# Second recurrent mixer of a two-block model: products of the rate phase moved from VectorE to GpSimd, on one core

## The chip, the cores and the metric

One core of a Trainium2 chip runs the whole program. The metric is the device time of one launch in microseconds, the median over repeated runs.

## The reference, cut to what matters

The program computes two blocks in float32. The second block has three mixers side by side; the second of them is a recurrent one ("rwkv7"), run forwards and backwards over 256 context and 512 latent tokens (768 columns in all). Before its scan it computes, for each direction d, a decay, a sigmoid `a`, a key `k_d` and a removal key `hd(a) * kk`; the readout at the end uses the sum of both directions' keys for a bonus term:

```
for d, (wd, ad) in enumerate(((wdf, adf), (wdb, adb))):
    w = -softplus(-(w0[d] + tanh(wd) @ w_up[d])) - 0.5
    decay = exp(-exp(w))
    a = sigmoid(a0[d] + ad @ a_up[d])
    k_d = k * (1.0 + (a - 1.0) * k_a)
    dirs.append((hd(decay), hd(k_d), hd(a) * kk))
...
bonus = (sum(r * (k_f + k_b) * r_k, axis=-1, keepdims=True) * v)
```

What follows (a chunked form of the scan, the output projection, then a mixture of 32 experts) is untouched.

## The kernel before

All tiles have 128 partitions. A feature tile of this mixer holds two halves m = 0, 1 (two heads each) of 768 columns: `kk` (normalised key), `k_` (key), `ak` (first the sigmoid `a`, then the removal key), `kd` (the key of the direction), `lw` (the sigmoid of the decay), `ci` and `ce` (running sums of `lw` within chunks of 128, with and without the own column), `e_tot` (the chunks' totals), `bias` (columns of the sums that centre later exponentials). `bonus` holds the latent part (512 columns) of the keys, summed over directions.

`rwkv_direction` (L3230) handles one direction. Its first stage is a weave of two programs: the chain of `rwkv_rates` (L3264) and `rwkv_decays` (L3324, with `rwkv_scores` L3591 woven into it), and as filler `early_project` (L1586), a part of the output projection (multiplications L1608, additions to x by VectorE L1615, weights loaded by the SP queue). `weave` (L395) opens a stage with barriers at both ends and writes each engine's instructions in the order of the fractions that the programs yield. The chain is put together by `in_turn` (L106): at the end of a part each of its computing engines drains and adds to the semaphore "ended", and every engine that has work in the next part waits until all have:

```
if i:
    eng.wait_ge(sem["ended"], sum(len(c) for c in computing[:i]))
...
    eng.drain().then_inc(sem["ended"], 1)
```

The engines of one stage share an order of work only by semaphores. `Chain` (L52), called `link`, makes an engine wait for the instruction that it has just issued, so that the next one may read its result.

In `rwkv_rates` TensorE multiplies four times (L3276), ScalarE takes sigmoids (L3287) into `lw` and `ak`, and VectorE makes the running sums (L2449), then per half the key of the direction in two steps (L3300 tensor_scalar, L3301 scalar_tensor_tensor), one product of both halves of `ak` with `kk` (L3302), the bonus (L3304 a copy in direction 0, L3306 an addition in direction 1), and per half the totals (L3309, a copy of 6 columns) and differences or sums of 768 columns (L3311 in direction 0; L3313 and L3314 in direction 1), last four small biases (L3318, L3319). GpSimd has nothing in it. In `rwkv_decays` ScalarE starts with L3350 and VectorE with L3332; L3338 reads `ak`, the transposes of TensorE (L3374) wait for it, and GpSimd's first work is L3718 of `rwkv_scores`, beside VectorE's L3673 and L3674.

Lines of other stages that are named below: L771 and L775 (VectorE, rotary products of the first block) and L253 (GpSimd, sums of weights there), L225 and L2239 (GpSimd products), L1797 and L2131 (GpSimd copies), L2611 (VectorE, tensor_scalar of 768 columns) and L2631 (VectorE, the copy of totals) in the first mixer.

Of the kernel before, what the change touches and what calls it, by code (L numbers as in the profile page):

```python
# [16 lines left out]
ALU = mybir.AluOpType  # L17
# [5 lines left out]
CTX = 256  # L23
# [1706 lines left out]
def over_heads(ap, n=HD):  # L1730

    shape = list(ap.shape) + [n]
    return ap.unsqueeze(len(ap.shape)).broadcast_to(shape)
# [712 lines left out]
def running_sums(nc, K, dve, link, lw, cum, tiles):  # L2446

    for t in tiles:
        link(nc.vector.tensor_tensor_scan(cum[:, t], K.reset[:], lw[:, t], 0.0, ALU.mult, ALU.add))  # L2449


def chunks(ap):

    return ap.rearrange("p (c n) -> p c n", n=P)
# [775 lines left out]
def rwkv_direction(nc, K, d, up_w, r_, k_, p_mix, kk, v_T, bonus, y, filler, rep, end):  # L3230
# [10 lines left out]
    with ExitStack() as p2:  # L3241
        kd, ak, lw = sb("kd", [P, 2, T2], p2), sb("ak", [P, 2, T2], p2), sb("lw", [P, 2, T2], p2)
        both = sb("c", [P, 2, 2, T2], p2)
        ce, ci = both[:, 0], both[:, 1]
        bias = sb("bias", [P, 2, 2, 3 * NCH], p2)
        chain = in_turn(
            (15, rwkv_rates(nc, K, d, up_w, p_mix, kk, k_, kd, ak, lw, ci, ce, e_tot, bias, bonus, range(4))),
            (54, rwkv_decays(nc, K, kk, r_, kd, ak, lw, ci, ce, at, kke, koT, re, e_tot, range(6),
                             rwkv_scores(nc, K, d, r_, kk, kd, ak, both, bias, at, bt, cd, (lw[:], p_mix[:, 4:6]), p_mix[:, 8], range(6)))))
        weave(nc, f"ru{d}", chain, filler)  # L3250
# [13 lines left out]
def rwkv_rates(nc, K, d, up_w, p_mix, kk, k_, kd, ak, lw, ci, ce, e_tot, bias, bonus, banks):  # L3264

    rows = slice(d * HD, (d + 1) * HD)
    border = HD - 1 if d == 0 else HD
    pieces = ((0, S), (S, CTX))

    def tensor(eng, sem):  # L3270
        for j in range(4):
            yield j / 8
            if j >= 2:
                eng.wait_ge(sem["sig"], j - 1)
            for x, (at_, n) in enumerate(pieces):
                ins = nc.tensor.matmul(K.psum[:, banks[2 * (j % 2) + x], :n], up_w[rows, j // 2, (j % 2) * P:(j % 2 + 1) * P],  # L3276
                                       p_mix[rows, 6 + j // 2, at_:at_ + n], start=True, stop=True)
            ins.then_inc(sem["up"], 1)

    def scalar(eng, sem):  # L3280
        eng.preload_act_table_set(SIGMOID)
        for j in range(4):
            yield (j + 0.5) / 8
            eng.wait_ge(sem["up"], j + 1)
            first = 10 + 4 * (j // 2) + 2 * d + j % 2
            for x, (at_, n) in enumerate(pieces):
                ins = nc.scalar.activation((lw, ak)[j // 2][:, j % 2, at_:at_ + n], K.psum[:, banks[2 * (j % 2) + x], :n], ACT.Sigmoid, bias=K.rw[:, first:first + 1])  # L3287
            ins.then_inc(sem["sig"], 1)
        eng.preload_act_table_set(LOG_EXP)

    def vector(eng, sem):
        link = Chain(eng, sem["v"])
        for m in range(2):
            yield 0.2 + 0.1 * m
            eng.wait_ge(sem["sig"], m + 1)
            running_sums(nc, K, eng, link, lw, ci, [m])
        yield 0.5
        for m in range(2):
            eng.wait_ge(sem["sig"], 3 + m)
            link(nc.vector.tensor_scalar(kd[:, m], ak[:, m], -1.0, K.rw[:, 6 + m:7 + m], ALU.add, ALU.mult))  # L3300
            link(nc.vector.scalar_tensor_tensor(kd[:, m], kd[:, m], 1.0, k_[:, m], ALU.add, ALU.mult))  # L3301
        link(nc.vector.tensor_tensor(ak[:], ak[:], kk[:], ALU.mult))  # L3302
        if d == 0:
            nc.vector.tensor_copy(bonus[:], kd[:, :, CTX:])  # L3304
        else:
            nc.vector.tensor_tensor(bonus[:], bonus[:], kd[:, :, CTX:], ALU.add)  # L3306
        yield 0.8
        for m in range(2):
            link(nc.vector.tensor_copy(e_tot[:, m], chunks(ci[:, m])[:, :, P - 1]))  # L3309
            if d == 0:  # L3310
                link(nc.vector.tensor_tensor(ce[:, m], ci[:, m], lw[:, m], ALU.subtract))  # L3311
            else:
                link(nc.vector.tensor_tensor(chunks(ce[:, m]), over_heads(e_tot[:, m], P), chunks(ci[:, m]), ALU.subtract))  # L3313
                link(nc.vector.tensor_tensor(ci[:, m], ce[:, m], lw[:, m], ALU.add))  # L3314
        middle = ci.rearrange("p m (c n) -> p m c n", n=HD)[:, :, :, 31]
        edge = ci.rearrange("p m (c n) -> p m c n", n=P)[:, :, :, border]
        for x, rate in enumerate((-RATE, RATE)):
            nc.vector.tensor_scalar(bias[:, x, :, 0:2 * NCH], middle, rate, None, ALU.mult)  # L3318
            nc.vector.tensor_scalar(bias[:, x, :, 2 * NCH:3 * NCH], edge, rate, None, ALU.mult)  # L3319

    return Program(["up", "sig", "v"], tensor=tensor, scalar=scalar, vector=vector)


def rwkv_decays(nc, K, kk, r_, kd, ak, lw, ci, ce, at, kke, koT, re, e_tot, banks, scores):  # L3324
# [1208 lines left out]
```

## Time and profile before

| | us |
|---|---|
| median of 3 runs (lowest, highest) | 2134.77 (2133.16, 2139.09) |
| the profiled execution | 2135.21 |
| its span in the trace | 2133.0 |
| busy: TensorE, VectorE, ScalarE, GpSimd | 1978.6 (93%), 987.5 (46%), 619.2 (29%), 354.7 (17%) |
| mean granted TensorE clock, share of full | 0.966 |

The profiled execution's time is 2.2 us more than its span, for what lies around the first and the last instruction. Busy shares are averages over stages. The timeline lists instructions by their start in us from the beginning of the span, with the idle time of the engine before them and what ended it; PE is TensorE, PEld its weight loads, DVE VectorE, ACT ScalarE, POOL GpSimd, and a q behind a name means the engine's sequencer (waits, drains, branches).

### The profile page before, as it was taken

The numbers are of one execution on the slowest core, as the hardware profiler recorded it, in microseconds if no ns is written. First come the engines' busy times: TensorE is split into PE (matmuls) and PEld (weight loads), VectorE is DVE, ScalarE is ACT, GpSimd is POOL, SyncE is SP. The second block draws the span as 40 slices with busy tenths as digits, with TensorE's granted clock in tenths as the row PEclk, the third lists the DMA queues.
The fourth block names the chain that finished last, engine by engine and source line by source line (L and its number), as shares of the span: only waits on it lengthen the run. The fifth ranks groups of instructions, "written<-read, shape, count | busy, mean of one in ns | idle before, by whom it ended". The sixth has DMA issues, their size and how long they took to land. (4 is left out here: it accounts for less than half of the span.)

```text
span 2133.0 us, 32611 instructions
## 1 busy us (share of the span) xinstructions
PE 1978.6 (93%) x13378; PEld 1387.4 (65%) x13378; DVE 987.5 (46%) x1954; ACT 619.2 (29%) x1311; POOL 354.7 (17%) x301
## 2 busy tenths in 40 slices
PE   7999999988999999998998898897899999999996
PEld 5885768856566576686996654684795555445542
DVE  5772075724452425478635777748743222111013
ACT  4551162131122212443123165326213111111111
POOL 5442103202220233341003100201300000000001
PEclk9999999979899999999999999899899999999999
DMA  4222201200001873121113110000018999999997
GB/s 168 89 83 79 79 18 51 71 25 30 30 27 40 330 290 135 40 79 31 41 46 118 32 37 30 2 2 31 3 30 349 396 426 427 426 425 426 428 427 314
DMA packets 51795, 325.84 MB, mean 153 GB/s; under 512 B 6464, under 2 KB 9152, under 8 KB 33344
## 3 DMA queue, kind: packets, MB, share of 16 engines
q1 hardware_dynamic: 50352, 319.03, 38.1%
q0 software_dynamic: 1152, 4.19, 0.5%
q8 instruction: 108, 1.77, 0.3%
q10 hardware_dynamic: 144, 0.52, 0.1%
q14 instruction: 39, 0.32, 0.0%
HBM read 311.67 MB, written 9.96 MB: 151 GB/s over the span
## 5 line engine op out<-in xcount | busy, mean ns | idle before, releaser
L3992 PE MATMUL psum<-m_ring,m_xg 128*64 128x512 f32 x944 | 207.1, 593 | 8.9 <-DMA m_ring<-in_w_in 8.9
L3992 PEld LDWEIGHTS psum<-m_ring,m_xg 128*64 128x64 f32 x944 | 68.4, 137 | 143.7 <-issue 143.6
L3974 PEld LDWEIGHTS psum<-m_sel,m_htok 128*128 128x128 f32 x1024 | 118.3, 194 | 13.7 <-issue 12.2
L3974 PE MATMUL psum<-m_sel,m_htok 128*128 128x128 f32 x1024 | 122.7, 279 | 1.4 <-DVE m_sel L3965 1.4
L3998 ACT ACTIVATE rstd<-psum 64x512 f32<-64x512 f32 x32 | 18.8, 588 | 302.8 <-PE psum L3992 288.3
L4002 DVE TENSOR_TENSOR m_hid<-rstd,psum 64x512 f32<-64x512 f32 x32 | 22.1, 691 | 171.6 <-ACT rstd L3998 171.5
L4017 PE MATMUL psum<-m_ring,m_hid_t 128*64 128x512 f32 x432 | 96.4, 596 | 2.3 <-DMA m_ring<-in_w_down 1.6
L4089 POOL DMA_INDIRECT m_ring<-expert_rows,m_pos x8 | 8.7, 1088 | 478.1 <-DMA expert_rows<-tmp 476.0
L289 PE MATMUL psum<-h,wring 128*128 128x256 f32 x336 | 82.9, 391 | 3.8 <-POOL n_v L262 1.9
L444 PE MATMUL psum<-wring,h 128*128 128x128 f32 x704 | 83.5, 277 | 0.7 <-ACT n_k L350 0.5
L829 PE MATMUL psum<-wring,h 128*128 128x512 f32 x192 | 82.6, 592 | 0.0
L444 PEld LDWEIGHTS psum<-wring,h 128*128 128x128 f32 x704 | 80.2, 192 | 2.6 <-ACT n_k L350 0.9
L746 ACT ACTIVATE tmp<-gatedB 32x512 f32<-32x512 f32 x96 | 60.3, 628 | 62.6 <-DVE gatedB L357 61.4
L289 PEld LDWEIGHTS psum<-h,wring 128*128 128x128 f32 x336 | 65.2, 196 | 19.2 <-issue 8.1
L829 PEld LDWEIGHTS psum<-wring,h 128*128 128x128 f32 x192 | 51.6, 269 | 30.5 <-issue 15.1
L1331 PE MATMUL psum<-h,wring 128*128 128x512 f32 x128 | 66.4, 650 | 0.8 <-ACT rstd L1341 0.8
L4017 PEld LDWEIGHTS psum<-m_ring,m_hid_t 128*64 128x64 f32 x432 | 29.5, 137 | 57.1 <-issue 51.9
L289 PE MATMUL psum<-v,folds 128*128 128x256 f32 x264 | 60.6, 379 | 0.1
L4023 DVE TENSOR_TENSOR tmp<-psum,rows 128x512 f32<-128x512 f32 x16 | 11.1, 691 | 106.2 <-DMA expert_rows<-tmp 102.6
L289 PE MATMUL psum<-x,wring 128*128 128x256 f32 x240 | 57.0, 380 | 2.0 <-DVE g_xc L357 2.0
L3965 DVE TENSOR_TENSOR m_sel<-m_rank,m_count 128x256 f32<-128x256 f32 x32 | 12.2, 421 | 99.9 <-PE psum L3974 99.6
L3983 ACT ACTIVATE m_xg<-psum,mod,gains 128x128 f32<-128x128 f32 x128 | 48.0, 459 | 30.9 <-PE psum L3974 30.9
(761 smaller groups left out, 4212.0 us busy)
## 6 DMA issues: line engine op xcount, KB each, us to landing
m_ring<-in_w_in SPq DMA_DIRECT2D x59, 2048.0 KB, 27.4
m_ring<-in_w_down SPq DMA_DIRECT2D x54, 1024.0 KB, 27.5
wring<-in_w1f SPq DMA_DIRECT2D x60, 512.0 KB, 3.5
ada_ring<-in_w_ada SPq DMA_DIRECT2D x12, 2048.0 KB, 12.2
wring<-in_w2f SPq DMA_DIRECT2D x31, 512.0 KB, 3.4
x<-in_w_in SPq DMA_DIRECT2D x5, 2048.0 KB, 24.7
x<-in_w_down SPq DMA_DIRECT2D x10, 1024.0 KB, 30.0
expert_rows<-tmp SPq DMA_DIRECT2D x14, 512.0 KB, 28.3
```

The source lines that it names most:

```text
L289: m = nc.tensor.matmul(self.bank(q, name)[:, :CTX], lhs(k), rhs(k), start=(fresh and k == 0), stop=(k == half - 1), skip_group_check=True)
L444: return nc.tensor.matmul(place(t, out), lhs, rhs, start=(k == 0), stop=(k == KD - 1))
L746: m = nc.scalar.activation(K.tmp[to:to + quarter, t % 2], of[p0:p0 + quarter], ACT.Copy)
L829: m = nc.tensor.matmul(K.psum[:, banks[u]], tokens, weights[:, kk], start=(k == 0), stop=(k == KD - 1))
L1331: m = nc.tensor.matmul(K.psum[:, banks[i % 2]], ws.weights(first + i, k), (h, gated)[i % 2][:, k], start=(k == 0), stop=(k == nk - 1))
L3965: return nc.vector.tensor_tensor(W.sel[:, :, s], over_heads(rank_e, SLOTS), over_rows(slots, TT), ALU.is_equal)
L3974: m = nc.tensor.matmul(K.psum[:, GATHER + k // 4, at:at + n], h_tok[:, t, k * P:(k + 1) * P], W.sel[:, t].rearrange("p s n -> p (s n)")[:, ...
L3983: m = nc.scalar.activation(W.xg[:, k].rearrange("p s n -> p (s n)")[:, :n], K.psum[:, GATHER + k // 4, at:at + n], ACT.Identity, scale=pre ...
L3992: m = nc.tensor.matmul(K.psum[i * SLOTS:(i + 1) * SLOTS, UP + s], W.xg[:, k, s], w[i], start=(k == 0), stop=(k == KD - 1))
L3998: return nc.scalar.activation(W.sg[s][SLOTS:], K.psum[0:SLOTS, UP + s], ACT.Silu)
L4002: return nc.vector.tensor_tensor(W.hid[s * SLOTS:(s + 1) * SLOTS], W.sg[s][SLOTS:], K.psum[SLOTS:, UP + s], ALU.mult)
L4017: m = nc.tensor.matmul(K.psum[at, DOWN + dh], W.hid_t[:, f, at], w[:, f], start=(f == 0), stop=(f == FT - 1))
```

## The change

Per half, the product of `ak` and `kk` goes to GpSimd as soon as VectorE's tensor_scalar has read `ak` (semaphore "less"), and the bonus as soon as `kd` is ready (semaphore "keys"), copied or added per half. VectorE's two links in the key's steps become a wait on "less" and a signal "keys", and it goes on to the totals. The phase now has four computing engines for "ended".

```diff
         for m in range(2):
             eng.wait_ge(sem["sig"], 3 + m)
-            link(nc.vector.tensor_scalar(kd[:, m], ak[:, m], -1.0, K.rw[:, 6 + m:7 + m], ALU.add, ALU.mult))
-            link(nc.vector.scalar_tensor_tensor(kd[:, m], kd[:, m], 1.0, k_[:, m], ALU.add, ALU.mult))
-        link(nc.vector.tensor_tensor(ak[:], ak[:], kk[:], ALU.mult))
-        if d == 0:
-            nc.vector.tensor_copy(bonus[:], kd[:, :, CTX:])
-        else:
-            nc.vector.tensor_tensor(bonus[:], bonus[:], kd[:, :, CTX:], ALU.add)
+            nc.vector.tensor_scalar(kd[:, m], ak[:, m], -1.0, K.rw[:, 6 + m:7 + m], ALU.add, ALU.mult).then_inc(sem["less"], 1)
+            eng.wait_ge(sem["less"], m + 1)
+            nc.vector.scalar_tensor_tensor(kd[:, m], kd[:, m], 1.0, k_[:, m], ALU.add, ALU.mult).then_inc(sem["keys"], 1)
         yield 0.8
...
-    return Program(["up", "sig", "v"], tensor=tensor, scalar=scalar, vector=vector)
+    def gpsimd(eng, sem):
+        yield 0.5
+        for m in range(2):
+            eng.wait_ge(sem["less"], m + 1)
+            nc.gpsimd.tensor_tensor(ak[:, m], ak[:, m], kk[:, m], ALU.mult)
+        yield 0.8
+        for m in range(2):
+            eng.wait_ge(sem["keys"], m + 1)
+            of = kd[:, m, CTX:]
+            if d == 0:
+                nc.gpsimd.tensor_copy(bonus[:, m], of)
+            else:
+                nc.gpsimd.tensor_tensor(bonus[:, m], bonus[:, m], of, ALU.add)
+
+    return Program(["up", "sig", "less", "keys", "v"], tensor=tensor, scalar=scalar, vector=vector, gpsimd=gpsimd)
```

## Rows read from the trace of the kernel before

**Rows 1.** Timeline, direction 0: start us, us, engine, line, operation, tiles, count [idle <-releaser].

```profile
1306.22 0.62 DVE L3300 TENSOR_SCALAR r_kd<-r_ak,vecs 128x768 f32<-128x768 f32 x1
...
1306.88 0.96 DVE L3301 SCALAR_TENSOR_TENSOR r_kd<-r_kd,p_mix 128x768 f32<-128x768 f32 x1
...
1309.52 1.76 DVE L3302 TENSOR_TENSOR r_ak<-r_ak,late 128x1536 f32<-128x1536 f32 x1
1311.31 0.69 DVE L3304 COPY r_bonus<-r_kd 128x1024 f32<-128x1024 f32 x1
1311.92 0.16 DVE L3309 COPY r_etot<-r_c 128x6 f32<-128x6 f32 x1
...
1313.32 0.96 DVE L3311 TENSOR_TENSOR r_c<-r_c,r_lw 128x768 f32<-128x768 f32 x1
...
1314.81 1.48 ACT L3350 ACTIVATE r_kke<-r_c 128x1536 f32<-128x1536 f32 x1 [6.92 <-DVEq L128]
```

**Rows 2.** Timeline, direction 1.

```profile
1450.89 1.76 DVE L3302 TENSOR_TENSOR r_ak<-r_ak,late 128x1536 f32<-128x1536 f32 x1
1452.68 1.22 DVE L3306 TENSOR_TENSOR r_bonus<-r_bonus,r_kd 128x1024 f32<-128x1024 f32 x1
1453.83 0.16 DVE L3309 COPY r_etot<-r_c 128x6 f32<-128x6 f32 x1
...
1458.70 1.48 ACT L3350 ACTIVATE r_kke<-r_c 128x1536 f32<-128x1536 f32 x1 [9.43 <-DVEq L128]
```

**Rows 3.** Single lines of GpSimd: duration in ns (min/median/max), first and last start, shape.

```profile
L2239 POOL TENSOR_TENSOR g_pool<-g_pool,const x8: 1260/1268/1272, 503.8 to 551.9; 128x512 f32<-128x512 f32 x8
...
L225 POOL TENSOR_TENSOR x<-h x1: 2353/2353/2353, 163.4 to 163.4; 128x1024 f32<-128x1024 f32 x1
...
L1797 POOL COPY g_pool<-level x1: 397/397/397, 559.0 to 559.0; 128x256 f32<-128x256 f32 x1
...
L2131 POOL COPY x<-g_g x1: 1887/1887/1887, 469.8 to 469.8; 128x2048 f32<-128x2048 f32 x1
```

**Rows 4.** Timeline, the first block at 31 to 35 us.

```profile
31.22 1.64 DVE L775 TENSOR_TENSOR qk<-qk,tmp 128x512 f32<-128x512 f32 x1
...
32.39 1.60 POOL L253 TENSOR_TENSOR folds<-folds,wring 128x512 f32<-128x512 f32 x1
...
32.79 1.75 DVE L771 TENSOR_TENSOR qk<-gatedB,rstd 128x512 f32<-128x512 f32 x1
```

**Rows 5.** Timeline, the phase behind the rates, direction 0.

```profile
1321.77 1.59 POOL L3718 TENSOR_TENSOR r_lw<-r_kd,p_mix 128x256 f32<-128x256 f32 x1 [124.91 <-DVE r_at L3338]
...
1326.23 1.02 POOL L3718 TENSOR_TENSOR r_lw<-r_kd,p_mix 128x256 f32<-128x256 f32 x1 [2.46 <-ACT p_mix L3636]
1326.24 0.42 DVE L3673 TENSOR_TENSOR r_lw<-r_ak,p_mix 128x256 f32<-128x256 f32 x1
...
1326.58 0.82 DVE L3674 TENSOR_TENSOR r_lw<-r_ak,p_mix 128x128 f32<-128x128 f32 x1
```

**Rows 6.** Single lines of VectorE, columns as in rows 3.

```profile
L775 DVE TENSOR_TENSOR qk<-qk,tmp x24: 691/1368/3110, 31.2 to 175.4; 128x512 f32<-128x512 f32 x24
...
L2611 DVE TENSOR_SCALAR h_k<-h_k,vecs x4: 619/1082/1510, 907.8 to 936.5; 128x768 f32<-128x768 f32 x4
...
L2631 DVE COPY h_etot<-h_c x2: 171/614/1056, 952.8 to 955.9; 128x6 f32<-128x6 f32 x2
```

**Rows 7.** Stretches: length, then busy us per engine (x instructions), PEclk, DMA share, GB/s.

```profile
1309.50:1314.80 5.30, 0.00 (x0) 0.00 (x0) 5.06 (x10) 0.00 (x0) 0.00 (x0) 0.75 0.00 0
1314.80:1318.40 3.60, 3.56 (x4) 1.52 (x5) 3.53 (x3) 3.22 (x4) 0.00 (x0) 0.50 0.03 7
1321.70:1325.00 3.30, 3.05 (x25) 2.81 (x26) 3.30 (x5) 2.43 (x7) 2.00 (x2) 1.00 0.00 0
1451.00:1458.70 7.70, 0.00 (x0) 0.00 (x0) 7.40 (x12) 0.00 (x1) 0.00 (x0) 0.79 0.00 0
1458.70:1462.30 3.60, 3.58 (x5) 1.51 (x6) 3.54 (x3) 3.23 (x4) 0.00 (x0) 0.50 0.00 0
```

## The prediction

> **What bounds the kernel now.** Over the whole span TensorE is the busy engine, 93% against 46% for VectorE and 17% for GpSimd (the table above), but that is an average over stages, and the change touches two short phases: the rates of direction 0, at about 1300 to 1315 us, and those of direction 1, at about 1441 to 1459 us. I therefore read the timeline of these two phases first, then looked for places where GpSimd and VectorE already work at once, and last at TensorE's clock around the phases.
>
> In the timeline the reader is to see who is late. After the projections and sigmoids only VectorE works: from 1306.22 one instruction follows the other, the second difference (L3311) ends at 1314.28, four small biases follow, and ScalarE's first instruction of the next phase (L3350) starts at 1314.81, 0.53 after that difference, having had 6.92 us of idle time that VectorE ended [rows 1]. In direction 1 the same ScalarE line starts at 1458.70 after 9.43 us of idleness that VectorE ended [rows 2]. TensorE does nothing from 1309.5 to 1314.8 and from 1451 to 1458.7 [rows 7]. So each microsecond of VectorE in this phase is a microsecond of the kernel, and the phase boundary (every computing engine adds to "ended", everyone waits) hands it on whole. GpSimd is free: its first work in the next phase (L3718) is where VectorE's L3338 is what it waits for, 124.91 us of idle time before it [rows 5]. That is the case for the move. The case against it is that the moved instructions read SBUF, as does nearly all that stays on VectorE.
>
> **What goes away on VectorE.** In direction 0 the product of ak and kk (L3302) starts at 1309.52 and the first copy of totals (L3309) at 1311.92: 2.40 us start to start, for L3302 (1.76) and L3304 (0.69) [rows 1]. In direction 1 it is 1450.89 to 1453.83: 2.94 us for L3302 (1.76) and L3306 (1.22) [rows 2]. Together 5.34. Two waits of VectorE on itself also fall away per direction. A linked instruction starts 0.03 to 0.04 us after its predecessor ends (L3301 at 1306.88 after 1306.84), an unlinked one 0.08 before it (L3309 at 1311.92, the copy before it ends at 1312.00) [rows 1]: 0.1 us each, 0.2 per direction, 0.4 in all.
>
> **What comes to GpSimd.** Per direction two products over 128x768 and two bonus operations over 128x512. A GpSimd product of 512 columns takes 1.27 us and one of 1024 takes 2.35 [rows 3], so 2.11 ns per column and 1.27 + 256 x 2.11 ns = 1.81 for 768. Its copy takes 0.397 for 256 columns and 1.887 for 2048 [rows 3], so 0.83 ns per column and 0.61 for 512. Direction 0: 2 x 1.81 + 2 x 0.61 = 4.84. Direction 1, where the bonus is a sum, 2 x 1.81 + 2 x 1.27 = 6.16. The Trainium skill (GPSIMD Engine Reference, Performance versus the Vector engine) gives some 2.6 cycles per column for two inputs at 1.2 GHz, an estimate of 1.66 us for 768 columns; by it each of the four would be 0.15 shorter, 0.6 in all, and the sum below +2.6. The rows' durations are the ones used.
>
> **Do they run side by side?** The trace answers this. VectorE's L775, a product of two 512-column SBUF operands, takes 0.691 at its shortest [rows 6]. With GpSimd at work L775 takes 1.64 and L771 1.75, and GpSimd's L253 takes 1.60 in place of 1.27 [rows 4]. The ends tell how: L775 ends at 32.86, L253 at 33.99, 1.13 later; L771 then ends at 34.54, 0.55 later. Each ends its own duration less 0.14 after the other's end. That is turn by turn, with 0.14 of start-up hidden, and not a common slowing. The stage right behind the rates shows it too: GpSimd's L3718, the same product each time, takes 1.59 at 1321.77 and 1.02 at 1326.23, by what VectorE has under way; L3674, that comes while it lasts, takes 0.82, although L3673 with twice its columns takes 0.42 [rows 5]. So VectorE's next instruction doesn't pass a GpSimd one that already waits. The one-input forms are no exception: the tensor_scalar of 128x768 takes 0.62 free and up to 1.51 beside GpSimd, and the tiny copy of totals, 128x6, took 1.06 instead of 0.17 [rows 6]. So totals, differences, sums and both steps of kd all meet GpSimd in turns.
>
> The Trainium skill (SBUF — State Buffer, Who interferes with whom) states that VectorE and GpSimd share a port pair, that whoever starts first holds it for the whole instruction and the other fully blocks. That rule speaks against this change. The trace agrees on the turns, but it hides 0.14 us at each hand-over; blocking with nothing hidden would give +5.7 us in place of the sum below. The measurement decides.
>
> **Schedule of direction 0** (end times; "held" ends at the end before it plus its duration less 0.14). Tensor_scalar m0 1306.84. L3301 m0 starts at 1306.88, before GpSimd has reacted, and ends 1307.84. GpSimd product m0, held, 1309.51. Tensor_scalar m1, held, 1309.99. L3301 m1 1310.99. GpSimd product m1 1312.66. Totals m0 1312.69. GpSimd bonus copy m0 1313.16. Difference m0 1313.98. GpSimd copy m1 1314.45. Totals m1 1314.48, difference m1 1315.48, and 0.53 from there to the next phase as now: 1316.0 in place of 1314.81. **+1.2 us.**
>
> **Direction 1.** Tensor_scalar m0 1448.22 (as long before L3302's old start as in direction 0), L3301 m0 1449.21, GpSimd product m0 1450.88, tensor_scalar m1 1451.36, L3301 m1 1452.36, GpSimd product m1 1454.03, totals m0 1454.06, GpSimd sum m0 1455.19, L3313 m0 1456.01, GpSimd sum m1 1457.14, L3314 m0 1457.96, totals m1 1458.16, L3313 m1 1459.16, L3314 m1 1460.16, next phase at 1460.7 in place of 1458.70. **+2.0 us.**
>
> As a check: 4.84 + 6.16 of GpSimd time, less 5.34, less some 17 hand-overs at 0.14 (2.4), is +3.2. The dropped waits give nothing here, since VectorE stands behind GpSimd at that moment. The ends of this term, by rows: nothing contended, -5.34 - 0.4 = -5.7 (GpSimd would finish at about 1311.7 and 1454.4, ahead of VectorE at 1312.1 and 1455.5, so it is covered); nothing hidden, 11.00 - 5.34 = +5.7. I take +3.2, since the rows with the same forms show turns with 0.14 hidden.
>
> **The small edits.** GpSimd now drains and adds to "ended", and the count waited for rises by one. In the schedule it ends 1 us and 3 us before VectorE, which hides it; with that cover gone it costs a hand-over of about 0.1. The new wait of VectorE on "less" has the place of the old link. Behind GpSimd's waits nothing else is queued in these phases, and no DMA moves: SP's weight loads and the output projection's multiplications keep their place. I take 0, between -0.1 and +0.3 for both directions.
>
> **TensorE's clock.** During the idle time it falls; from the restart it is granted 0.50 (1.2 GHz) for 3.6 us in both directions, after 5.3 us of idleness and after 7.7 [rows 7]. A longer pause before it changes nothing in that, and at 1321.7, where the transposes on the path begin, it is at 1.00 again (2.4 GHz). The matmuls in the slow stretch are the output projection's and are not waited for. I take 0.
>
> **Sum.** 2135.21 (profiled execution, span 2133.0) + 3.2 = 2138.4. The median of the runs shown, 2134.77, is 0.4 lower, so I expect a median of **2138.0**, +0.15%. About 0.3% (6.4 us) is what a measurement of this kernel can tell from no change; the three runs of before span 5.9 us alone.
>
> **Rivals.**
> (a) Turns as forecast, between nothing hidden and some extra hiding, +1 to +5.7: 2136 to 2140.5. Chance 0.81.
> (b) The instructions fit beside each other: -5.7, 2129.1. For it: the engines have no data in common but two handed-over tiles, and L3718 beside one-input work isn't slowed everywhere. Against it are the turns, for each of the forms that stay on VectorE [rows 4 to 6]. It decides if L3301 and L3311 keep 0.96 us beside a GpSimd product. Chance 0.08; it would be a gain of 0.27%, so about half of it would be read as faster.
> (c) Half of it: contention for the products only, while the totals and differences run beside the bonus work; GpSimd 2 x 3.62 = 7.24 less 5.34 less 8 hand-overs (1.1) = +0.8: 2135.6. Against it is the 1.06 us copy [rows 6]. Chance 0.07.
> (d) Slower past the bound: TensorE's pause, lengthened by 1.2 and 2.0, keeps the low clock until the transposes at 1321.7 and 1465.6. PE is busy 3.05 us in that stretch at full clock [rows 7]; at half it would be about twice that, +3 per direction, 2138.0 + 6 = 2144. It decides if the granted clock is still 0.50 more than 6.9 us after the restart. Against it: 3.6 us after either pause. Chance 0.04.
>
> **How the numbers follow.** (a) is the likeliest and sets 2138.0. The range takes in (a), (c) and the spread of runs on either side of their median (-1.6, +4.3), and leaves out (b) and (d): 2131.5 to 2142.0. Faster by over 0.3%: half of (b), 0.04. Slower by over 0.3%: (d) and the top of (a) with a high run, 0.05. Within: 0.91.
>
> **What would show it.** Right: GpSimd's products last 2.3 to 2.7 us where they arrive behind L3301 (1.81 alone); tensor_scalar of m1 lasts over 2 us instead of 0.62; the copy of totals of m0 about 1.7 instead of 0.16; L3350 starts about 1.2 and 2.0 us later after the phase's first sigmoid. Wrong: L3301, L3311, L3313 and L3314 at 0.96 throughout and L3350 2.6 to 3.1 earlier; or GpSimd as the engine that L3350 waits for; or any change of length in a stage outside the two phases.

## The result, and the profile after

The changed kernel takes 2136.74 us in the median of 20 runs (2133.05 to 2142.28) and the kernel before 2131.14 in 20 runs (2125.29 to 2139.09); the ratio is 1.0019 with a 95% interval of 1.0010 to 1.0028. That is slower by 2 to 6 us, and within the 0.3% that the prediction called no change. The median of before is now 3.6 us under that of the first three runs, so the ratio (+0.15% forecast, +0.19% measured) says more than a comparison of 2136.74 with the forecast 2138.0.

The profiled execution took 2135.00 us (span 2132.8; before 2133.0). Two single executions can't be set against each other by their spans: in this one the first running sum of the phase came almost 5 us earlier than in the profile of before, with nothing changed ahead of it. The phases themselves can. The busy shares first, from section 1 of the page after: GpSimd has eight instructions more and 15.5 us more busy time, VectorE four fewer and yet 2.8 us more, because an instruction that waits for its turn is recorded as running, as the rows below show.

```profile
PE 1979.3 (93%) x13378; PEld 1388.3 (65%) x13378; DVE 990.3 (46%) x1950; ACT 619.5 (29%) x1311; POOL 370.2 (17%) x309
```

The timeline of direction 0 of the changed kernel, columns as in rows 1 (L3302 is now the second key step, L3305 the totals, L3307 the difference, L3321 GpSimd's product, L3327 its bonus copy, L3360 ScalarE's first instruction of the next phase):

```profile
1301.30 0.62 DVE L3300 TENSOR_SCALAR r_kd<-r_ak,vecs 128x768 f32<-128x768 f32 x1
...
1301.95 0.96 DVE L3302 SCALAR_TENSOR_TENSOR r_kd<-r_kd,p_mix 128x768 f32<-128x768 f32 x1
1302.00 2.58 POOL L3321 TENSOR_TENSOR r_ak<-r_ak,late 128x768 f32<-128x768 f32 x1 [107.73 <-DVE r_kd L3300]
...
1302.83 2.16 DVE L3300 TENSOR_SCALAR r_kd<-r_ak,vecs 128x768 f32<-128x768 f32 x1
...
1305.03 0.96 DVE L3302 SCALAR_TENSOR_TENSOR r_kd<-r_kd,p_mix 128x768 f32<-128x768 f32 x1
1305.07 2.57 POOL L3321 TENSOR_TENSOR r_ak<-r_ak,late 128x768 f32<-128x768 f32 x1 [0.50 <-DVE r_kd L3300]
1305.90 1.77 DVE L3305 COPY r_etot<-r_c 128x6 f32<-128x6 f32 x1
1307.59 1.89 POOL L3327 COPY r_bonus<-r_kd 128x512 f32<-128x512 f32 x2
1307.70 1.30 DVE L3307 TENSOR_TENSOR r_c<-r_c,r_lw 128x768 f32<-128x768 f32 x1
1309.04 0.46 DVE L3305 COPY r_etot<-r_c 128x6 f32<-128x6 f32 x1
1309.54 0.96 DVE L3307 TENSOR_TENSOR r_c<-r_c,r_lw 128x768 f32<-128x768 f32 x1
...
1311.03 1.48 ACT L3360 ACTIVATE r_kke<-r_c 128x1536 f32<-128x1536 f32 x1 [8.07 <-DVEq L128]
```

The reader is to see the turns. GpSimd's first product comes 0.05 us behind L3302, lasts 2.58 instead of 1.81, and ends 1.66 after L3302 does. The tensor_scalar of m1, 0.62 in [rows 1], lasts 2.16; the copy of six columns of totals 1.77 instead of 0.16. From the first tensor_scalar to ScalarE's L3360 it is 9.74 us, where rows 1 have 8.59. The same in direction 1 (L3309, L3310 differences and sums, L3329 the bonus sum):

```profile
1447.84 2.16 DVE L3300 TENSOR_SCALAR r_kd<-r_ak,vecs 128x768 f32<-128x768 f32 x1
...
1450.91 1.77 DVE L3305 COPY r_etot<-r_c 128x6 f32<-128x6 f32 x1
1452.61 3.19 POOL L3329 TENSOR_TENSOR r_bonus<-r_bonus,r_kd 128x512 f32<-128x512 f32 x2
1452.71 1.97 DVE L3309 TENSOR_TENSOR r_c<-r_etot,r_c 128x768 f32<-128x768 f32 x1
1454.72 1.90 DVE L3310 TENSOR_TENSOR r_c<-r_c,r_lw 128x768 f32<-128x768 f32 x1
...
1459.35 1.48 ACT L3360 ACTIVATE r_kke<-r_c 128x1536 f32<-128x1536 f32 x1 [11.37 <-DVEq L128]
```

Here the phase takes 13.04 us in place of 11.10. The difference and the sum of m0 last 1.97 and 1.90 instead of 0.96, each behind one of GpSimd's bonus sums (two merged in the row, 3.19 together). The two phases give **+1.15 and +1.94, 3.1 us in all**.

Last TensorE's clock in the changed kernel, columns as in rows 7:

```profile
1311.05:1316.60 5.55, 5.54 (x7) 2.42 (x8) 5.51 (x4) 5.18 (x10) 0.00 (x0) 0.50 0.12 36
...
1317.80:1321.00 3.20, 2.84 (x24) 2.60 (x25) 3.20 (x6) 2.33 (x7) 2.01 (x2) 1.00 0.00 0
1400.00:1406.00 6.00, 6.00 (x32) 6.00 (x32) 0.00 (x0) 1.92 (x4) 0.00 (x0) 0.55 0.00 0
...
1459.36:1463.40 4.04, 4.04 (x5) 1.85 (x6) 4.00 (x3) 3.67 (x4) 0.00 (x0) 0.50 0.00 0
```

It is granted 0.50 for 5.6 us after the restart at 1311.06 in direction 0 and for 4.1 us after the one at 1459.37 in direction 1, and 1.00 when the transposes begin, 6.9 us after each restart. The longer low stretch isn't a mark of the change: in a second profile of the kernel before, direction 1 has it too, after a pause of the old length:

```profile
1454.47:1460.40 5.93, 5.92 (x7) 2.50 (x8) 5.88 (x4) 5.56 (x11) 0.00 (x0) 0.50 0.14 41
```

In the stretch at 1400 us the changed kernel's clock is near half as well, where the first profile of before has full clock:

```profile
1400.00:1406.00 6.00, 5.04 (x57) 4.80 (x57) 1.08 (x3) 1.82 (x4) 0.00 (x0) 1.00 0.00 0
```

### The profile page after: what moved, and what is told of

It is laid out like the page before. It is cut to its first block and busy times, and to the rows that moved or that the text cites. A ratio compares the mean times of both kernels' runs of the same rounds, so it can differ in the third digit from the quotient of the medians.

```text
span 2132.8 us, 32615 instructions
## 1 busy us (share of the span) xinstructions
PE 1979.3 (93%) x13378; PEld 1388.3 (65%) x13378; DVE 990.3 (46%) x1950; ACT 619.5 (29%) x1311; POOL 370.2 (17%) x309
## 3 DMA queue, kind: packets, MB, share of 16 engines
q8 instruction: 108, 1.77, 0.3%
## 5 line engine op out<-in xcount | busy, mean ns | idle before, releaser
L3984 PEld LDWEIGHTS psum<-m_sel,m_htok 128*128 128x128 f32 x1024 | 116.7, 192 | 13.7 <-issue 12.2
```

Source lines behind the costliest of these rows:

```text
L3984: m = nc.tensor.matmul(K.psum[:, GATHER + k // 4, at:at + n], h_tok[:, t, k * P:(k + 1) * P], W.sel[:, t].rearrange("p s n -> p (s n)")[:, ...
```

## The experiments

Every phase length below is taken from the start of the first tensor_scalar to ScalarE's first instruction of the next phase, unless the text says otherwise.

| kernel | direction 0 | direction 1 | both against before | ratio to before |
|---|---|---|---|---|
| before (three profiles) | 8.59 | 11.10 to 11.11 | | |
| changed (three profiles) | 9.73 to 9.74 | 13.04 | +3.1 | 1.0019 and 1.0023 |
| no GpSimd work | 5.95 | 7.93 | -5.8 | 0.9971 |
| GpSimd writes only | 6.16 | 8.14 | -5.4 | one execution |
| key alone on GpSimd | 9.70 | 12.22 | +2.2 | 1.0007 |
| bonus alone on GpSimd | 8.44 | 11.73 | +0.5 | 0.9997 |
| products cut in two | 9.53 | 12.76 | +2.6 | one execution |
| bonus late | 7.99 | 9.97 | -1.7 | 0.9985 |
| bonus late, key step on ScalarE | 6.84 * | 8.82 * | -4.1 | 0.9982 |

\* from the end of the second running sum, which before is 8.63 and 11.14.

**Leave GpSimd's work out.** The theory: the moved instructions and those left take turns at what the engines share. The rival: the new semaphores, GpSimd's wake-up and its drain cost the time.

```diff
         for m in range(2):
             eng.wait_ge(sem["less"], m + 1)
-            nc.gpsimd.tensor_tensor(ak[:, m], ak[:, m], kk[:, m], ALU.mult)
         yield 0.8
         for m in range(2):
             eng.wait_ge(sem["keys"], m + 1)
-            of = kd[:, m, CTX:]
...
-                nc.gpsimd.tensor_tensor(bonus[:, m], bonus[:, m], of, ALU.add)
```

> The changed kernel with its four GpSimd instructions per direction left out: the removal key isn't multiplied and the bonus stays zero (a zero-scaled copy stands in for the sigmoid of a, so that the numbers stay finite); the semaphores, GpSimd's waits and its part in 'ended' remain. The length of a phase is taken from the start of the first tensor_scalar (L3300 line) to ScalarE's first instruction of the next phase: 8.59 and 11.10 us before, 9.73 and 13.05 after. Theory (turns at a shared SBUF interface): with nothing to take turns with, VectorE's instructions last as alone, so 5.9 and 7.95 us; the whole kernel 5.8 us under the kernel before, a ratio of 0.997. Rival (the new semaphores, GpSimd's wake-up and its drain at the boundary cost the time): the phases stay near 9.7 and 13.0.

The diff leaves out two further edits: ScalarE writes zeros into `ak` by scaled copies in place of the second pair of sigmoids, and in direction 0 GpSimd clears `bonus` by a memset ahead of the phase. The kernel computes neither the removal key nor the bonus.

The phases took 5.95 and 7.93 us; the ratio is 0.9971 (0.9954 to 0.9989; 2127.29 against 2133.12 us). Its timeline in direction 0:

```profile
1303.37 0.96 DVE L3305 SCALAR_TENSOR_TENSOR r_kd<-r_kd,p_mix 128x768 f32<-128x768 f32 x1
...
1304.25 0.61 DVE L3303 TENSOR_SCALAR r_kd<-r_ak,vecs 128x768 f32<-128x768 f32 x1
...
1305.77 0.17 DVE L3308 COPY r_etot<-r_c 128x6 f32<-128x6 f32 x1
...
1308.67 1.48 ACT L3360 ACTIVATE r_kke<-r_c 128x1536 f32<-128x1536 f32 x1 [4.46 <-DVEq L128]
```

VectorE's tensor_scalar and totals last 0.61 and 0.17 again, and an instruction without a link behind it is overtaken by 0.08 us, as it was in rows 1. So the semaphores and the fourth engine at the boundary cost nothing that can be seen, and GpSimd's four instructions are the whole of the difference to the changed kernel: 3.8 us in direction 0 and 5.1 in direction 1.

**Let GpSimd write without reading.**

```diff
-            nc.gpsimd.tensor_tensor(ak[:, m], ak[:, m], kk[:, m], ALU.mult)
+            nc.gpsimd.memset(ak[:, m], 0.0)
```

and a memset in place of each bonus operation.

> The changed kernel with GpSimd's products, copies and sums replaced by memsets of the same tiles and columns: GpSimd has as many instructions at the same places, that write SBUF and read nothing (removal key and bonus become zero). Theory (turns for what GpSimd reads, against VectorE's second SBUF input): the scalar_tensor_tensor and the differences and sums keep 0.96 us although a memset runs beside them; at most the tensor_scalar and the copies of totals wait, and a memset of 768 columns is short, so the phases take 6.0 to 6.5 and 8.0 to 8.5 us. Rival (any GpSimd instruction holds VectorE up for its whole length): the scalar_tensor_tensor or the difference beside a memset is longer by its length, some 0.5 to 0.7 us each, and the phases take 7.5 and 9.5 or more.

6.16 and 8.14 us. The timeline of direction 0:

```profile
1305.16 0.96 DVE L3302 SCALAR_TENSOR_TENSOR r_kd<-r_kd,p_mix 128x768 f32<-128x768 f32 x1
1305.19 0.74 POOL L3321 MEMSET r_ak<- 128x768 f32 x1 [107.86 <-DVE r_kd L3300]
...
1306.68 0.96 DVE L3302 SCALAR_TENSOR_TENSOR r_kd<-r_kd,p_mix 128x768 f32<-128x768 f32 x1
1306.71 0.74 POOL L3321 MEMSET r_ak<- 128x768 f32 x1 [0.78 <-DVE r_kd L3300]
1307.39 1.01 POOL L3326 MEMSET r_bonus<- 128x512 f32 x2
1307.56 0.38 DVE L3305 COPY r_etot<-r_c 128x6 f32<-128x6 f32 x1
1307.97 0.96 DVE L3307 TENSOR_TENSOR r_c<-r_c,r_lw 128x768 f32<-128x768 f32 x1
```

A memset of 768 columns runs its whole 0.74 us inside VectorE's scalar_tensor_tensor, and neither is longer for it (memsets of 37 and 296 columns elsewhere in the kernel take 0.13 and 0.34 us, from which 768 columns are an estimate of 0.73). That refutes the rival that any GpSimd instruction holds VectorE up: for VectorE's instructions with two operands in SBUF it is GpSimd's reading that they take turns with. The copy of totals, though, lasts 0.38 instead of 0.17 beside the third memset. The Trainium skill (SBUF — State Buffer, Who interferes with whom) draws the line at this place: an instruction of VectorE with two SBUF inputs contends only with a GpSimd instruction that reads SBUF, while its two-port forms of copy and tensor_scalar contend with any. The trace agrees on two operands (0.96 beside a memset) and on the copy (0.38 beside the next); no tensor_scalar stood beside a memset in this run.

**One of the two moves alone.** In the first run the bonus is back on VectorE as one instruction of 1024 columns, in the second the removal key as one of 1536:

```diff
+        eng.wait_ge(sem["keys"], 2)
+        if d == 0:
+            nc.vector.tensor_copy(bonus[:], kd[:, :, CTX:])
+        else:
+            nc.vector.tensor_tensor(bonus[:], bonus[:], kd[:, :, CTX:], ALU.add)
```

```diff
+        eng.wait_ge(sem["keys"], 2)
+        link(nc.vector.tensor_tensor(ak[:], ak[:], kk[:], ALU.mult))
```

> Only the removal key on GpSimd; the bonus on VectorE as one instruction, as before. Theory (turns, each ending its own duration less 0.14 after the other): both products still stand in VectorE's way, 3.62 us less two hand-overs each for 1.76 taken off: phases of 9.8 and 12.3 us, +1.2 and +1.2 against before, so the bonus on GpSimd costs nothing in direction 0 and some 0.75 in direction 1. Rival (GpSimd's products run beside VectorE and only the bonus operations, that come last, hold up the end): phases of about 6.8 and 9.3, below before.

> Only the bonus on GpSimd; the removal key on VectorE as one instruction of 1536 columns, as before. Theory (turns): direction 0 exchanges 0.61 us of VectorE for two copies of 0.61 less hand-overs: 8.5 us, 0.1 under before; direction 1 exchanges 1.15 us for two sums of 1.27 less hand-overs: 11.75 us, +0.65 against before. Rival (side by side): 8.0 and 9.95.

The key alone: 9.70 and 12.22 us (ratio 1.0007, 0.9987 to 1.0026). In direction 1 the bonus sum of VectorE, 1.22 us by itself [rows 2], stands behind GpSimd's second product and lasts 2.71:

```profile
1453.12 2.57 POOL L3326 TENSOR_TENSOR r_ak<-r_ak,late 128x768 f32<-128x768 f32 x1 [0.50 <-DVE r_kd L3300]
1454.07 2.71 DVE L3307 TENSOR_TENSOR r_bonus<-r_bonus,r_kd 128x1024 f32<-128x1024 f32 x1
...
1461.57 1.48 ACT L3357 ACTIVATE r_kke<-r_c 128x1536 f32<-128x1536 f32 x1 [10.55 <-DVEq L128]
```

The bonus alone: 8.44 and 11.73 us (ratio 0.9997, 0.9980 to 1.0014). Its timeline in direction 1 has both sides waiting: GpSimd's second sum behind the key product (2.83 instead of 1.27), then the totals behind that sum (1.11 instead of 0.17):

```profile
1447.88 2.83 POOL L3327 TENSOR_TENSOR r_bonus<-r_bonus,r_kd 128x512 f32<-128x512 f32 x1 [0.89 <-DVE r_kd L3302]
1449.63 1.11 DVE L3307 COPY r_etot<-r_c 128x6 f32<-128x6 f32 x1
```

All four lengths are within 0.1 us of the turns and none is near the side-by-side values (6.8, 9.3, 8.0, 9.95). Put together, moving the key costs 2.2 us, moving the bonus as well 0.9 more.

**Cut the products in two.**

```diff
-            nc.gpsimd.tensor_tensor(ak[:, m], ak[:, m], kk[:, m], ALU.mult)
+            for at_ in (0, T2 // 2):
+                part = slice(at_, at_ + T2 // 2)
+                nc.gpsimd.tensor_tensor(ak[:, m, part], ak[:, m, part], kk[:, m, part], ALU.mult)
```

> The changed kernel with each of GpSimd's products cut into two of 384 columns (four instructions of 1.0 us in place of two of 1.81). Theory (strict turns, each taking over 0.14 us before the other's end as recorded): VectorE comes in between the pieces; total GpSimd time grows by 0.19 per cut, but each cut adds hand-overs that hide 0.14 twice: phases from the first tensor_scalar of 9.5 and 12.85 us instead of 9.74 and 13.04. Rival (GpSimd keeps the interface while it has instructions queued): the second piece follows the first at once, VectorE waits as long as before plus the start-up, and the phases take 10.1 and 13.4.

9.53 and 12.76 us, by the theory. VectorE gets its turn between the pieces:

```profile
1298.41 0.96 DVE L3302 SCALAR_TENSOR_TENSOR r_kd<-r_kd,p_mix 128x768 f32<-128x768 f32 x1
1298.45 5.65 POOL L3323 TENSOR_TENSOR r_ak<-r_ak,late 128x384 f32<-128x384 f32 x4 [107.80 <-DVE r_kd L3300]
...
1299.28 1.35 DVE L3300 TENSOR_SCALAR r_kd<-r_ak,vecs 128x768 f32<-128x768 f32 x1
...
1300.67 1.63 DVE L3302 SCALAR_TENSOR_TENSOR r_kd<-r_kd,p_mix 128x768 f32<-128x768 f32 x1
```

GpSimd's four pieces are merged in one row here (5.65). The tensor_scalar of m1 lasts 1.35, not 2.16. L3302 behind it now waits too (1.63), and still the phase is 0.21 and 0.28 us shorter with more instructions. The rule of the turns accounts for most of it: a cut costs GpSimd 0.19 us more and adds two hand-overs that hide 0.14 each, so two cuts per direction are worth -0.18.

**Where GpSimd's work does fit: the bonus late, and a step for ScalarE.** Both start from the kernel before. The bonus goes to the end of the scores, behind the last factors:

```diff
             nc.gpsimd.tensor_tensor(kc[:, x, 1], kd[:, :, es], ekc[:, x], ALU.mult).then_inc(sem["pooled"], 1)
+        eng.wait_ge(sem["factors"], NCH)
+        if d == 0:
+            nc.gpsimd.tensor_copy(bonus[:], kd[:, :, CTX:])
+        else:
+            nc.gpsimd.tensor_tensor(bonus[:], bonus[:], kd[:, :, CTX:], ALU.add)
```

> The kernel before, with the bonus alone taken out of the rate phase and given to GpSimd at the end of the scores that follow (after the last factors are ready), where VectorE's remaining products read PSUM and one SBUF operand. Theory (turns only where both read SBUF through the shared interface): the phases, from the end of the second running sum to ScalarE's first instruction of the next phase, go from 8.63 and 11.14 to 8.0 and 9.95 us; VectorE's products beside the bonus keep 0.42 and 0.68 us and the stage ends where it did: 1.8 us under the kernel before, a ratio of 0.9992, too little to be certain in the time of the whole. Rival (GpSimd's work holds VectorE up wherever it stands): the stage of the scores is longer by 1.0 us in direction 0 and 2.3 in direction 1, and nothing is won.

7.99 and 9.97 us from the first tensor_scalar, 8.02 and 10.00 from the running sum. The stage behind, from ScalarE's first instruction to the start of the inversion, takes 40.85 and 41.60 us, the same as before to 0.01. The timeline of direction 1 there:

```profile
1486.55 0.86 DVE L3657 TENSOR_TENSOR r_at<-psum,const 64x256 f32<-64x256 f32 x2
...
1486.60 2.36 POOL L3720 TENSOR_TENSOR r_bonus<-r_bonus,r_kd 128x1024 f32<-128x1024 f32 x1 [4.26 <-DVE p_mix L3674]
...
1487.34 0.67 DVE L3661 TENSOR_TENSOR r_cd<-psum,const 128x512 f32<-128x512 f32 x1
...
1487.93 0.67 DVE L3661 TENSOR_TENSOR r_bt<-psum,const 128x512 f32<-128x512 f32 x1
...
1488.53 0.67 DVE L3661 TENSOR_TENSOR r_cd<-psum,const 128x512 f32<-128x512 f32 x1
```

GpSimd's sum of 1024 columns takes 2.36 us (2.35 alone, [rows 3]) while VectorE does five products with one operand in PSUM, and they keep 0.43 (two merged: 0.86) and 0.67. In direction 0 the copy of 1024 columns takes 1.04 us, and VectorE's same five products 0.85 for two and 0.68 to 0.69. The rival has nothing here. The ratio is 0.9985 (0.9972 to 0.9998), more than the 1.7 us account for (0.9992), which is inside the interval.

The second run adds to this (not shown: a small instruction of VectorE that prepares the negated k_a, and that VectorE now does the product of `ak` and `kk` per half, right behind the second key step and without links):

```diff
+            if j >= 2:
+                eng.wait_ge(sem["sig"], j + 1)
+                eng.wait_ge(sem["negated"], 1)
+                m = j - 2
+                nc.scalar.activation(kd[:, m], ak[:, m], ACT.Identity, scale=K.rw[:, 6 + m:7 + m], bias=K.rw[:, m:m + 1]).then_inc(sem["less"], 1)
...
-            link(nc.vector.tensor_scalar(kd[:, m], ak[:, m], -1.0, K.rw[:, 6 + m:7 + m], ALU.add, ALU.mult))
```

> As the run with the late bonus, and the first step of the key (a tensor_scalar on VectorE) goes to ScalarE as an activation of a times k_a minus k_a right behind each sigmoid, with 768 columns each. ScalarE idles in this phase and has its own access to SBUF. Theory: VectorE loses two instructions of 0.62 and their waits per direction: 6.7 and 8.7 us from the end of the second running sum, 4.4 us under the kernel before, a ratio of 0.998. Rival: the second key step waits for ScalarE, whose sigmoids and steps are in one queue and end about 1.9 us after the running sums: phases of 7.5 and 9.5.

6.84 and 8.82 us, 0.1 over the forecast: ScalarE's step takes 1.03 us and VectorE waits 0.28 us for the first, while its own instructions beside ScalarE's keep 0.95 to 0.96. The ratio is 0.9982 (0.9973 to 0.9990), 2128.87 against 2131.75 us. It is the fastest of the kernels here that compute everything, 0.4% under the changed one; from the run with the late bonus alone it can't be told apart in the time of the whole, only in the phases.

**The rest of the difference.** The phases give 3.1 us, a ratio of 1.0015, which is inside the measured interval, though the measured ratio is a little higher. Apart from what lies ahead of the first phase, the stretch that differs most between the two profiles is the one from the start of the inversion of direction 0 to the end of the second running sum of direction 1, 91.90 us before and 94.38 after.

> The changed kernel once more, unchanged, beside the two runs above. In its first profile TensorE ran at half clock for some 6 us in the stage behind the inversion of direction 0 (1400 to 1406 us), where the profile of before shows full clock. If that comes by chance, the dip is absent here or elsewhere and the ratio to the kernel before is 1.0015, which is what the two phases give (3.1 us). If the change brings it on, the dip stands at the same place again and the ratio is 1.002 to 1.003.

> The changed kernel a third time: 94.4 to 94.6 us in the rest of direction 0 if the stretches of half clock are set by the kernel, anything from 90.3 to 94.6 if not. The two rate phases take 9.77 and 13.08 us in either case.

> The kernel before once more, for the length of the rest of direction 0 (from the start of the inversion to the end of the second running sum of direction 1): 91.90 us in the profile of before, 94.38 and 94.59 in two of the changed kernel, 90.3 to 94.6 in the variants. If the stretches of half clock in it follow from how long the pause before was, this profile has 91.9 again. If they come by chance, it can be anything from 90.3 to 94.6.

> The same a third time: 91.9 again if the stretches of half clock are set by the kernel, anything from 90.3 to 94.6 if not. The two rate phases take 8.63 and 11.14 us in either case.

The changed kernel again gave a ratio of 1.0023 (1.0013 to 1.0032). Phases: the same in every profile, to 0.01 us. The stretch: 94.38, 94.59 and 94.37 in the changed kernel, 91.90, 95.27 and 91.61 in the one before, 90.2 to 94.6 in the variants so far. The second profile of before shows a reduced clock in the same place:

```profile
1400.00:1406.00 6.00, 6.00 (x46) 6.00 (x45) 0.43 (x1) 2.33 (x4) 0.00 (x0) 0.79 0.01 3
```

The traces give the price of this. The rows are the 40 us that begin 20 us after the start of the inversion, in the first profile of before, in its second, and in the changed kernel (the clock is the third number from the end):

```profile
1375.70:1415.70 40.00, 36.64 (x715) 34.57 (x710) 24.02 (x64) 13.01 (x29) 7.99 (x11) 1.00 0.01 3
...
1368.10:1408.10 40.00, 37.04 (x671) 35.51 (x666) 22.36 (x61) 11.55 (x27) 7.74 (x11) 0.87 0.01 3
...
1371.90:1411.90 40.00, 37.12 (x659) 35.69 (x655) 22.39 (x60) 11.59 (x27) 7.28 (x10) 0.87 0.01 3
```

The length of the stretch follows the time that TensorE spends at 0.50 in it: 90.2 to 90.3 us with 13.7 us at 0.50 (the products cut in two, GpSimd writing only or doing nothing), 91.6 to 91.9 with 17.1 (two profiles of before, the late bonus), 93.3 with 20.5 (the bonus alone), 94.4 to 94.6 with 23.9 (the changed kernel each time, the key alone, ScalarE's step), 95.3 with 27.1 (the second profile of before). That is some 0.4 us for each microsecond at 0.50; the two dips that the rows at 0.87 have, 10.2 us together, cost about 4 us.

What brings the dips on stays open. The kernel before can have them too (one profile of three), so the change isn't needed for them. But the changed kernel has them in all three, at the same places to 0.1 us, and so has the key alone, whose direction 0 is almost as long; the kernel with ScalarE's step, the fastest of all, has them as well. By the signs written down ahead, the repeats of the changed kernel spoke for a cause in the kernel and the repeats of the one before against it. Three profiles of each don't tell whether the change makes the dips likelier; the mean of the stretch is 1.5 us higher after.

> The changed kernel with idle multiplications on TensorE (128x128, result unused, a free bank) behind the projections of each rate phase, 50 and 76 of them, so that its pause of 6.7 and 10.0 us is all but filled. Theory: the phases stay at 9.77 and 13.08 us, since VectorE and GpSimd set them; the granted clock stays at 1.00 in the pause and behind it; if the extra stretch at half clock behind the inversion of direction 0 hangs on that pause, the rest of direction 0 falls from 94.4 to about 91 us and the kernel comes within 0.1% of the one before. Rival (that stretch has its cause in the inversion itself): it stays at 94.4 and the ratio at 1.002.

```diff
             ins.then_inc(sem["up"], 1)
+        yield 0.99
+        beats(nc, K, 5, (50, 76)[d])
```

This run went wrong as an experiment. A float32 multiplication of this shape is two entries in the trace, so that 50 of them took 11.3 us and not 5.9, and TensorE became the engine that the boundary waits for:

```profile
1304.00 11.33 PE L1744 MATMUL psum<-const 128*128 128x128 f32 x100
...
1310.78 0.17 DVE L3317 TENSOR_SCALAR r_bias<-r_c 128x12 f32<-128x12 f32 x1
1315.38 1.49 ACT L3362 ACTIVATE r_kke<-r_c 128x1536 f32<-128x1536 f32 x1 [12.46 <-PEq L128]
```

ScalarE's idle time was ended by TensorE, the phases took 14 and 20 us, and the ratio is 1.0102 (1.0085 to 1.0118). One thing can still be read from it: with full clock throughout 1300 to 1320 us the stretch behind took 95.7 us, with 27.0 at 0.50 in it, so filling the pause doesn't keep the inversion from its own slow clock.

## Why the prediction was right

- **The phases and VectorE at their end.** Right: ScalarE, TensorE and VectorE start the next phase 0.06 to 0.12 us after VectorE's last bias, before and after the change, and the stage behind keeps its length, so what a phase gains or loses is passed on whole.
- **What is taken off.** 5.34 us and 0.4 for the links, 5.7 in all. With nothing on GpSimd the phases shrank by 2.64 and 3.17, 5.8.
- **Durations on GpSimd.** 1.81 for 768 columns could not be seen undisturbed, but 1.66 after the other's end is 1.81 less 0.15. The copies of 512 took 0.61 by the row that had no turn to wait for, the sum 1.255 instead of 1.27. By the Trainium skill's 2.6 cycles per column (GPSIMD Engine Reference, Performance versus the Vector engine), an estimate of 1.66 us for the product, it would have ended 1.52 after. The trace has 1.66, so the row was the better source.
- **Turns with 0.14 hidden.** This is the step that carries the sum, and it held at each instruction: all ends of the two schedules are met to 0.1 us. Counted from the first tensor_scalar, the schedule had GpSimd's first product end at 3.29 us (3.28 measured), the second tensor_scalar at 3.77 (3.70), GpSimd's second product at 6.44 (6.35), the totals 6.47 (6.38), the first difference 7.76 (7.71), the second 9.26 (9.20). The forecast is a little too long mainly for the tensor_scalar, of which more than 0.14 is hidden behind the product (0.20). +1.2 and +2.0 were forecast, +1.15 and +1.94 came, and so did the other signs that were named: 2.58 for GpSimd's product, 2.16 for the tensor_scalar, 1.77 for the totals. The rough check beside it counts 17 hand-overs; the schedules have 16, which would give +3.4, so its +3.2 agrees in part by that miscount.
- **The rival side by side** (b) falls: L3307, L3309 and L3310 did not keep 0.96 beside GpSimd. Half of the sign that was named for it was badly chosen, though: the second key step (L3301, now L3302) did keep 0.96 beside GpSimd's product, because it starts first each time, and it is the product and the tensor_scalar behind it that are longer (2.58 and 2.16). **Contention for the products only** (c) falls by what stood beside the bonus work: the second totals (0.46 instead of 0.17), the differences and the sum (1.30, 1.97, 1.90).
- **TensorE's clock** at 0: right in the outcome, wrong in the reading. The low stretch after the restart isn't 3.6 us in both directions: the first profile of before has 4.1 and 3.6, the other two 3.1 and 6.0, 4.0 and 3.8, and the changed kernel 5.6 and 4.1, 5.7 and 3.9, 5.7 and 4.1. It follows the length of the pause in no order that these show. **The lasting low clock** (d) falls because the transposes begin 6.9 us after the restart in every profile of the two kernels; with 6.0 us the margin was 0.9, less than the prediction took it to be.
- **The small edits** at 0: confirmed by the run without GpSimd's work.
- **The total.** +3.2 forecast for the phases, +3.1 found, +4.0 (2.1 to 6.0) measured in the kernel. The excess is inside the interval; if it is real, the dips of the clock behind the inversion are the candidate that was not in the sum. They alone move a single execution by as much as the change does, so it is the phases, and not the time of the whole, that confirm the sum. One sign of being wrong did appear to the letter, a change of length outside the two phases (91.90 to 94.38); the second profile of before, at 95.27, shows that it needs no change. That the median came within 1.3 us of 2138.0 is partly luck, since the level of the kernel before fell by 3.6. And the range doesn't follow from the terms named for it: (c) less 1.6 is 2134.0, and (a) plus 4.3 is 2142.3 to 2144.8, where 2131.5 to 2142.0 stands.

## What to carry to other kernels

In these runs GpSimd's time was worth something to VectorE only beside products that take one operand from PSUM and one from SBUF. Beside instructions with two SBUF operands, and beside copies and tensor_scalars within SBUF, what GpSimd reads and computes is done in turns, at GpSimd's longer durations, and the phase grows by their sum, less VectorE's time that is taken off and less what the two engines' start-ups hide. So before moving an elementwise instruction across, look in the trace for the two engines' rows one above the other, take the ends and not the durations, and write the schedule out turn by turn. The same bonus that cost time beside two-operand work was free some 35 us later beside products out of PSUM, and ScalarE took a step of the same chain without making any of VectorE's instructions longer.

## What the runs showed that was not expected

- Cutting each of GpSimd's products in two made the phases shorter, by 0.21 and 0.28 us, with more instructions.
- A recorded duration on either engine includes the wait for the turn: VectorE's busy time rose by 2.8 us while 5.4 us of work was taken off it.
- A six-column copy waits behind a memset that writes only (0.38 us instead of 0.17), while a product of two operands and 768 columns doesn't (0.96).
- The kernel before (in one profile of three) and the changed one (in all three) have two dips to half clock behind the inversion, 10.2 us together, that cost about 4 us, as much as the whole effect of the change. They stood there also when TensorE worked through the pause ahead.
